# Hybrid block and mixture of experts on one core: slots, router logits, first unit, diagonal store, last expert's loads and output placed anew

## The reference

```python
def second_block(x, ...):
    ...
    x = x + jnp.concatenate([y_pool, y_diff], axis=-1) @ w_out[l]
    x = x + cross_attention(rms_norm(x, xattn_norm_g[l]), rms_norm(mem, mem_norm_g[l]),
                            w_cq[l], w_ckv[l], w_co[l])
    x = x + moe_ffn(rms_norm(x, ffn_norm_g[l]), w_router[l], b_router[l], w_gu[l], b_gu[l],
                    w_down[l], b_down[l])
    return rms_norm(x, final_norm_g)

def moe_ffn(h, w_router, b_router, w_gu, b_gu, w_down, b_down):
    logits = (xt @ w_router + b_router).astype(jnp.float32)
    top_val, top_idx = lax.top_k(logits, TOP_K)
    gates = jax.nn.softmax(top_val, axis=-1)
    ...
        hb = clamped_swiglu(xb @ w_gu[e] + b_gu[e])
        yb = hb @ w_down[e] + b_down[e]
        return yb * g[:, None].astype(yb.dtype)
```

## Time and profile before

| | |
|---|---|
| median of three runs | 1724.79 us (1724.74 to 1726.17) |
| the profiled execution's own time | 1726.6 us |
| its span | 1724.8 us |
| busy share of the span: PE, PEld, DVE, ACT, POOL | 92%, 58%, 44%, 28%, 11% |
| HBM read, written | 524.70 MB, 1.62 MB |
| mean HBM rate over the span | 305 GB/s |

### The profile page before, as it was taken

How to read it: one execution, slowest core, us unless ns; L and a number is a source line. 1 busy time by engine, 2 the same in 40 slices (tenths; PEclk the granted TensorE clock), 3 DMA queues, 4 the chain that set the end, 5 groups by cost and what they waited for, 6 DMA issues and landing times.

```text
span 1724.8 us, 22680 instructions
## 1 busy us (share of the span) xinstructions
PE 1578.4 (92%) x9684; PEld 998.8 (58%) x9684; DVE 753.1 (44%) x1333; ACT 482.6 (28%) x825; POOL 182.2 (11%) x208
## 2 busy tenths in 40 slices
PE   7999999999999999989999988888898888889886
PEld 6998899999999989973333322223232322323221
DVE  6798777979884788551221211111121212111121
ACT  4245666455553564530110101010010101001001
POOL 0201102515530041020000000000000000000000
PEclk9999999999999999999999999999999999999999
DMA  9866455556655635658999999999999999999996
GB/s 219 173 206 167 120 135 175 165 171 192 178 194 174 197 117 189 247 199 331 422 421 422 421 421 421 420 421 421 421 421 421 421 422 422 420 421 421 422 421 270
DMA packets 195002, 527.89 MB, mean 306 GB/s; under 512 B 18546, under 2 KB 136351, under 8 KB 145743
## 3 DMA queue, kind: packets, MB, share of 16 engines
q1 hardware_dynamic: 191008, 519.23, 78.8%
q0 software_dynamic: 3344, 6.93, 2.6%
q10 hardware_dynamic: 542, 0.21, 0.1%
HBM read 524.70 MB, written 1.62 MB: 305 GB/s over the span
## 4 chain that ended last, share of the span: by engine, by line
DMA 45%; PE 44%; DVE 7%; ACT 2%; issue 1%; SPq 0%; ACTq 0%; DVEq 0%
PE bank L604 43%; DMA slot_ring<-in_w_down 15%; DMA slot_late<-in_w_down 8%; DMA slot_high<-in_w_down 8%; DMA slot_memx<-in_w_down 8%; DVE slot_ring_r L1972 2%; DMA slot_ring<-in_w_gu 2%; DMA slot_memt<-in_w_gu 2%; DMA slot_ring<-in_w_in 2%; ACT high_r L1535 1%; DVE h_sb L1980 1%; DVE conv L1980 0%; DVE rstd L2014 0%; DVE stat L2190 0%; DVE stat L2408 0%
## 5 line engine op out<-in xcount | busy, mean ns | idle before, releaser
L604 PE MATMUL bank<-h_hi_r,high_r 128*128 128x256 f32 x1000 | 286.7, 287 | 7.7 <-DVE slot_ring_r L1972 3.4
L1972 DVE TENSOR_TENSOR slot_ring_r<-slot_ring,high_r 128x1024 fp32r<-128x1024 f32 x198 | 250.3, 1306 | 78.1 <-ACT high_r L1535 75.8
L604 PE MATMUL bank<-h_lo_r,high_r 128*128 128x256 f32 x1000 | 283.1, 283 | 0.0
L1976 DVE TENSOR_SCALAR ga<-bank 128x512 f32<-128x512 f32 x32 | 22.1, 691 | 591.1 <-PE bank L604 591.1
L604 PE MATMUL bank<-h_hi_r,slot_ring_r 128*128 128x256 f32 x952 | 269.5, 283 | 0.0
L1535 ACT ACTIVATE high_r<-slot_ring 128x1024 fp32r<-128x1024 f32 x198 | 198.0, 1051 | 64.2 <-PE bank L604 43.4
L604 PEld LDWEIGHTS bank<-h_hi_r,high_r 128*128 128x128 f32 x1000 | 191.3, 191 | 11.3 <-DVE h_lo_r L1972 4.3
L1535 ACT ACTIVATE th_e<-ga 128x512 f32<-128x512 f32 x32 | 20.2, 630 | 624.0 <-DVE ga L1976 624.0
L604 PEld LDWEIGHTS bank<-h_lo_r,high_r 128*128 128x128 f32 x1000 | 191.4, 191 | 0.1
L604 PEld LDWEIGHTS bank<-h_hi_r,slot_ring_r 128*128 128x128 f32 x952 | 182.2, 191 | 0.0
L604 PE MATMUL bank<-slot_ring,xg 128*64 128x512 f32 x528 | 124.6, 603 | 11.4 <-DMA slot_ring<-in_w_gu 11.4
(11 more groups left out here) (441 smaller groups left out, 2901.0 us busy)
## 6 DMA issues: line engine op xcount, KB each, us to landing
slot_ring<-in_w_gu SPq DMA_DIRECT2D x66, 1024.0 KB, 27.0
slot_high<-in_w_gu SPq DMA_DIRECT2D x50, 1024.0 KB, 26.7
slot_ring<-in_w_down SPq DMA_DIRECT2D x49, 1024.0 KB, 26.6
slot_last<-in_w_gu SPq DMA_DIRECT2D x38, 1024.0 KB, 27.1
slot_ring<-in_w_in SPq DMA_DIRECT2D x36, 1024.0 KB, 5.3
slot_late<-in_w_gu SPq DMA_DIRECT2D x32, 1024.0 KB, 26.7
slot_high<-in_w_down SPq DMA_DIRECT2D x25, 1024.0 KB, 27.0
slot_ring<-in_w_up SPq DMA_DIRECT2D x44, 512.0 KB, 4.8
```

Of the source, the lines that this page charges most:

```text
L604: return e.matmul(o, lhs, rhs, start=start, stop=stop, skip_group_check=True)
L1972: return e.tensor_tensor(o, i, j, op)
L1976: return e.tensor_scalar(o, i, s1, None, op1)
```

## The change

It has seven parts.

1. **Places in SBUF and DRAM.** `COLS` has 32 more columns, 128 bytes in each partition, which moves x, h, ring, high slots and `h_hi`; the table of constants in DRAM gets unused columns at its end.
2. **First unit.** `("ub", 0)` comes in four transfers, two for each half of k; ACT rounds the first half when the first two have landed (`early_in`).
3. **ACT's start.** The second group of row loads and the rounding of `wfc` stand behind the split of the next two units.
4. **Diagonal store.** Both stores go to ACT's queue, behind the copies of `qa`; on POOL's queue `lams`, `wrt`, `brt` and `pos_i` follow the first loads without a wait.
5. **Router.** DVE multiplies `wrt` by the gains in advance. PE multiplies it by x, not by h: blocks 0 to 3 ahead of the product of the last `co` unit, 4 to 7 behind it. The squares are summed to one column for each token block, root and reciprocal work on 128x2, and the factor is put in where logits and `h_tok` are copied out of PSUM. ACT makes h as x times gain. x_tok comes by halves of the channels.
6. **DVE's splits in `add_residual`.** One `ahead((w, 3))` behind the loop in place of those inside it for i of 2 and 3.
7. **Last expert and output.** SP loads all eight `gu` units of expert 31 in one run, then the `dn` units of 30 and of 31. ACT squares all four output blocks; sums, root, reciprocal and scaling are made for each block of 128 tokens.

```diff
+    parts["unused"] = np.zeros((P, -(sum(a.shape[1] for a in parts.values()) - 3) % P))
...
-        CONST, COLS = 0, -(-n_const // 8) * 8 + 64
+        CONST, COLS = 0, -(-n_const // 8) * 8 + 96
...
+        two_columns_halved(("ub", 0), w_in, OFF["ub"], OFF["ub"] + BR)
+        for c in range(1, BT):
...
+            for i in range(3):
+                co_unit(i)
+            banks.take(q, "router")
+            logits(range(0, 4))
+            co_unit(3)
+            pe.mark("moe")
+            turn_h(0)
+            banks.take(q, ("ffn_g", "sums"))
+            token_squares(0)
+            logits(range(4, KT)).then_inc(*pe.step("router"))
+            banks.give("router", (dve, "logits"))
+            token_squares(3).then_inc(*pe.step("sums", "ffn_g"))
...
+            for u in range(KT // 2):
+                down(q, NE - 2, u)
+                if u == 2:
+                    turn_hidden(q, NE - 1)
+            for u in range(KT // 2):
+                down(q, NE - 1, u)
+                if u == 1:
+                    scatter(q, NE - 2)
             scatter(q, NE - 1)
...
-                    if n and k >= 4:
-                        u = k - 4
-                        load_dn(q, n - 1, u, w_dn[n - 1, u * 256:(u + 1) * 256, :].rearrange("(p k) n -> p k n", p=P))
+                    if 0 < n < NE - 1 and k >= 4:
+                        load_dn(q, n - 1, k - 4)
+            for n in (NE - 2, NE - 1):
+                for u in range(KT // 2):
+                    load_dn(q, n, u)
...
-            q.wait_ge(*landed(("ub", 0)))
+            q.wait_ge(*early_in["early"])
             high(("ub", 0), 0)
...
                     squares(norm, squares_of(norm), x, i, dve["residual", w, i])
-                    if i >= 2:
-                        ahead((w, i))
+                ahead((w, 3))
...
                 if i == 2:
+                    q.wait_ge(*wrt_in["wrt"])
+                    gains = cols_sb[:, col_at["ffn_g"]:col_at["ffn_g"] + KT].rearrange("p (k o) -> p k o", o=1)
+                    tt(wrt, wrt, gains.broadcast_to([P, KT, NE]), ALU.mult).then_inc(*dve.step("router gains"))
...
-            apply("ffn_g", x, h)
...
+            out_squares(0)
+            out_squares(1)
+            out_squares(2)
+            out_root(0)
+            out_squares(3)
+            out_root(1)
...
+            out_sums(0)
+            out_factor(0)
+            q.wait_ge(*fg_in["fg"])
+            out_part(0)
+            out_sums(1)
+            out_part(1)
+            out_factor(1)
+            out_part(2)
+            out_part(3)
```

More of the change, by code:

```diff
@@ L1043, in tensor_program, with co_unit, logits, token_squares @@
             pe.mark("ffn start")
[L1044 to L1055, removed]
+            def co_unit(i):
+                project(("co", i), mix_s, lambda k: dve["co split", k // 2], (dve, ("residual", "co", i)))
+            def logits(ks):
+                q.wait_ge(*dve["router gains"])
+                for k in ks:
+                    q.wait_ge(*dve["residual", "co", k // 2])
+                    m = matmul(bank("router")[k % 4 * NE:(k % 4 + 1) * NE, 0:S], wrt[:, k, :], x[:, k, :], k < 4, k >= 4)
+                return m
+            def token_squares(i):
+                q.wait_ge(*sq_by("ffn_g", i)["square", "ffn_g", i])
+                q.wait_ge(*pool["squares", "ffn_g"])
+                for t in range(TT):
+                    for k in (2 * i, 2 * i + 1):
+                        m = matmul(bank(("ffn_g", "sums"))[:, t:t + 1], sq_last[:, k, t * P:(t + 1) * P], ones[:, 0:1],
+                                   k == 0 and t == 0, k == KT - 1)
+                return m
             def turn_back(name, src, t, c, *until):
@@ L1062, in turn_back, with turn_h @@
                 banks.give((name, t, c), *until)
+            def turn_h(c):
+                for t in range(TT):
+                    q.wait_ge(*act["gained", 4 * c + 3])
+                    turn_back("h_tok", h, t, c, (act, ("h_tok hi", t, c)), (dve, ("h_tok lo", t, c)))
+            for i in range(3):
[10 more added lines that the diff above has]
+            token_squares(3).then_inc(*pe.step("sums", "ffn_g"))
+            banks.give(("ffn_g", "sums"), (act, ("root", "ffn_g")))
+            q.wait_ge(*act["logit rows"])
+            for t in range(TT):
+                m = matmul(bank("router")[:, S + t * NE:S + (t + 1) * NE], mean_sb[:, t * P:(t + 1) * P], C("stack"), True, True)
+            m.then_inc(*pe.step("logits turned"))
+            turn_h(1)
             for c in range(2):
                 for t in range(TT):
[L1066 to L1073, removed]
                     turn_back("x_tok", x, t, c, (act, ("x_tok", t, c)))
@@ L1620, in scalar_program @@
                 ahead(name)
+                if c == 0:
+                    load_rows(1)
+                    q.wait_ge(*wfc_in["wfc"])
+                    af(wfc_s.hi, wfc, ACT.Copy).then_inc(*act.step("wfc hi"))
                 q.wait_ge(*pe[name])
@@ L1750, in add_residual @@
                     if i % 2:
-                        squares(norm, h, x, i, dve["residual", w, i])
+                        squares(norm, squares_of(norm), x, i, dve["residual", w, i])
+                    if norm == "ffn_g":
+                        q.wait_ge(*dve["residual", w, i])
+                        for k in (2 * i, 2 * i + 1):
+                            af(h[:, k, :], x[:, k, :], ACT.Copy, scale=col("ffn_g", k)).then_inc(*act.step("gained", k))
                 ahead((w, 3))
@@ L2506, in vector_program @@
             least = spread(top8[:, :, TOPK - 1:TOPK])
+            q.wait_ge(*act["root", "ffn_g"])
+            e.reciprocal(token_norm, token_norm).then_inc(*dve.step("token factors"))
             q.wait_ge(*pe["logits turned"])
             q.wait_ge(*brt_in["brt"])
-            tt(logit, bank("router")[:, S:S + TT * NE].rearrange("p (t n) -> p t n", t=TT),
-               brt.rearrange("p (o n) -> p o n", o=1).broadcast_to([P, TT, NE]), ALU.add).then_inc(*dve.step("logits"))
+            own()
+            for t in range(TT):
+                stt(logit[:, t, :], bank("router")[:, S + t * NE:S + (t + 1) * NE], token_norm[:, t:t + 1], brt, ALU.mult,
+                    ALU.add).then_inc(*dve.step("logits"))
             own()
```

96 lines of the change are left out of this document (52 added, 44 removed).

## The result

The median after the change is 1707.43 us (1706.8 to 1707.67, four runs) against 1725.48 us (1724.74 to 1729.96, four runs); the ratio is 0.9889, with a 95% interval of 0.9872 to 0.9907. That is 18 us less, where 7.5 were forecast: right in direction, wrong in size. The profiled execution after took 1707.46 us with a span of 1705.7.

A forecast was written before the change was run, and what follows sets the result against it. Engine work bounds the kernel up to about 800 us, then the DMA stream of expert weights, lastly final products and output. Terms sum to -7.45 us: 1719.15 from the profiled 1726.6, or 1717.3 on the median's scale; range 1712 to 1722.

The forecast's parts named there:

- What bounds the kernel: Up to about 800 us engine gains move all that follows; then bytes and rate count; at the end, last products and output.
- Experts, 0 between -3 and +5: Stream of expert weights: unit sizes and nearly all the order kept, eight of fifteen slots moved by 128 bytes; taken as 0.
- The single comparison: Loads into one slot at another offset landed in 27.2 us, the ring's in 27.0; read as saying nothing of offsets.
- the favourable rival: Moved slots speed the expert stream, 1% on them gaining 4.8 us, to some 1712 us; chance 0.05.
- Start, -1.3: Kernel start: halved first unit and ACT's queue order give -2.9 us, early small loads cost 1.6; between -3 and +0.5.
- the wait, -1.9: PE's wait of 1.94 us before 87.96, for a slow unit load, goes whole as small loads leave that stretch.
- ln2, +0.65: End of layer 1's attention: splits queued ahead of the next pair delay the reciprocal by about 0.65 us.
- Cross attention, -1.6: Residual loop there: split moved behind the residual, which starts about 2.0 us earlier; -1.6 us, between -3.4 and -0.5.
- Router, -2.2: Router's products need only x, half go ahead at 1.7 us on PE's path; counts at 766.1, not 768.27; -3.5 to 0.
- End, -1.1: Last products end some 0.35 us earlier by load order; the last output scaling begins 0.78 us earlier.
- The slower rivals: Diagonal store slower on ACT's queue, up to 1731.2 us, chance 0.10; moved slots slow the stream, chance 0.03.
- the third: Rival: small loads cost the start 4 us and the router gives nothing; 1721.9 us, chance 0.15.

The follow-up runs named there:

- the test of DVE's order: The changed kernel with DVE's split put back inside the residual loop; one run, 1703.5 us.
- the fastest version: The changed kernel with the small loads behind the first unit's rounding and the end slots at a multiple of 512 bytes; 1702.1 us, ratio 0.9857.

## Why the prediction was wrong, point by point

**What bounds the kernel: right.** What was gained before 790 us was carried through: the stream's length followed its rate, and not the time at which it began. That very reading said that 1% of rate is 9.5 us, more than all the other terms; it should have made the rate the first thing to price.

**Experts, 0 between -3 and +5: the step that failed.** It measured -10.9 us, first gate copy to last landing. The failed step is "a difference that says nothing of offsets. I take 0". The single comparison had no aligned slot in it. And the bound of -3 had no row under it; the favourable rival got 0.05 and a price of 4.8 us for 1% on the moved slots, when seven aligned slots of fifteen lift the whole stream by 1.2%. The direction of the total was right by terms that held, but most of its size came from this one, which no term had.

**Start, -1.3, and the wait, -1.9: sum right (-3.0 measured), parts not.** The small loads cost 2.8 and not 1.6 us. The start gave about 1 us in the end: PE's first product came 1.55 later, but the 1.45 us of idle time ahead of 27.40 and the wait at 86 us are gone. The wait went whole, for the store's sake and not for the small loads'; its 1.94 us was one value of a wait that varied from 0.4 to 2.7, so how the 3.0 falls to the two terms is only known to about 1 us.

**ln2, +0.65: right** (+0.5). **Cross attention, -1.6: about right.** The row of the table has -1.65, of which the test of DVE's order shows 1.2. PE's idle time fell from 2.06 to 0.65 us, not under the 0.5 that was named as a sign. The four products behind it took 1.13 us at a granted clock of 1.00, where they had taken 1.71 at 0.63.

**Router, -2.2: too small** (-3.6). The term that was mis-sized is "3.39 / 2 = 1.7 us ... added to PE's path": it measured 0.64, and that is 1.1 of the 1.4 us by which the forecast fell short. The router's products stood behind an idle PE and ran at a granted clock of 0.57 in the window 760.2 to 763.7, 634 ns each in the median. Moved in between the co products they ran at 1.00 and took 391, all eight in 0.64 us. The row of the tile before (shortest, median and longest ns, then first and last start):

```profile
L604 PE MATMUL bank<-h_sb,wrt x16: 380/634/636, 760.3 to 763.3; 128*32 128x256 f32 x16
```

And after:

```profile
L618 PE MATMUL bank<-x_sb,wrt x16: 379/391/403, 743.3 to 751.7; 128*32 128x256 f32 x16
```

**End, -1.1: about right.** It gave 1.3 us up to the last scaling, of which 0.6 reach the end of the span; the load order's part is not shown.

**The slower rivals: none came.** Neither the store nor the slots slowed anything. Of the third, the small loads did cost the start 2.8 us, but the router gave more than forecast.

## What to carry to other kernels

Where a stream at the DMA limit fills most of the span, price its rate first, and look at where its destinations begin: seven of fifteen slots at a multiple of 256 bytes, where they had been 128 past one, were worth 1.2% here, for one constant. A control taken from the trace must differ in the property that is in question, not just in the number. And a product that is moved from behind an idle engine into a busy stretch is to be priced by rows of the busy stretch.

## What the runs showed of the hardware

**Slot offsets.** 1 MB loads in packets of 8 KB ran at 421 GB/s into slots at 128 past a multiple of 256 bytes (`h_hi` at 32 or 160) and at 426 to 427 once seven or fourteen of the fifteen began at one. Why was not tried.

**The clock between the picks and the first gate copy.** Over the 18 profiled executions, one of each kernel, this stretch took from 25.5 to 29.7 us, with the same instructions in all changed kernels. In the changed kernel, PEclk, the third number from the right, is 0.75, 1.00, 0.82, 0.67:

```profile
761.49:769.49 8.00, 7.85 (x35) 4.98 (x35) 3.02 (x12) 1.20 (x2) 0.30 (x1) 0.75 0.51 192
769.49:777.49 8.00, 8.00 (x44) 3.84 (x44) 0.00 (x0) 1.20 (x2) 0.00 (x0) 1.00 0.93 349
777.49:785.49 8.00, 7.88 (x25) 2.91 (x23) 1.43 (x4) 0.59 (x1) 0.00 (x0) 0.82 0.99 407
785.49:791.49 6.00, 6.00 (x22) 1.99 (x19) 1.57 (x4) 0.00 (x0) 0.00 (x0) 0.67 0.31 100
```

and in the fastest version 0.81, 1.00, 1.00, 1.00:

```profile
758.35:766.35 8.00, 7.86 (x38) 5.00 (x39) 3.02 (x12) 1.19 (x2) 0.30 (x1) 0.81 0.51 179
766.35:774.35 8.00, 8.00 (x43) 3.53 (x43) 0.00 (x0) 1.20 (x2) 0.00 (x0) 1.00 0.98 393
774.35:782.35 8.00, 7.89 (x31) 3.05 (x29) 2.41 (x6) 0.59 (x1) 0.00 (x0) 1.00 0.87 365
782.35:788.35 6.00, 5.76 (x30) 2.51 (x28) 2.67 (x4) 1.12 (x2) 0.30 (x1) 1.00 0.81 283
```

These 4 us are more than any single term of the prediction, so a single run of a kernel here can't rank it; what decides between the two was not found.

**Two stores on two queues.** 552 KB from eight partitions held the DMA engines twice as long on POOL's queue as on ACT's (141 against 72 us of engine time), though both took 10 to 11 us from the first packet to the last.
